# Expert results of a routed feed-forward layer: from one-hot scatter products and closing stores to accumulating indirect DMAs

## The reference, cut to what matters

```
def expert_choice_ffn(h, w_router, w_gate, w_up, w_down):
    ...
    aff = jax.nn.softmax((t @ w_router).astype(jnp.float32), axis=-1)
    gate, idx = lax.top_k(aff.T, cap)

    def expert(args):
        wg, wu, wd, ix, g = args
        xe = t[ix]
        he = jax.nn.silu(xe @ wg) * (xe @ wu)
        return (he @ wd) * g[:, None].astype(he.dtype)

    ye = lax.map(expert, (w_gate, w_up, w_down, idx, gate))
    y = jnp.zeros((n, D), h.dtype).at[idx.reshape(-1)].add(ye.reshape(-1, D))
...
x = x + expert_choice_ffn(rms_norm(x, norm2_g[l]), ...)
```

## Time and profile before

| | |
|---|---|
| median of 3 runs | 2422.82 us (2420.98 to 2423.57) |
| profiled execution, span | 2422.3 us |
| PE busy | 2308.2 us (95%) |
| PEld busy | 1983.5 us (82%) |
| DVE busy | 1764.9 us (73%) |
| ACT busy | 1390.5 us (57%) |
| POOL busy | 149.0 us (6%) |
| moved by DMA | 616.14 MB, 609.08 MB of it read from HBM |
| expert loop | from about 773 us to about 2404 us of the span |

### The profile page before, as it was taken

One profiled execution on the slowest core, in us unless ns is written; L12 is line 12 of the kernel. 1 busy time (PEld: TensorE's weight loads), 2 busy tenths in 40 slices (PEclk: granted clock), 3 DMA queues, 4 the chain that ended last, 5 costly groups with the idle time before them and its releaser, 6 DMA issues.

```text
span 2422.3 us, 32629 instructions
## 1 busy us (share of the span) xinstructions
PE 2308.2 (95%) x12576; PEld 1983.5 (82%) x12576; DVE 1764.9 (73%) x1571; ACT 1390.5 (57%) x1137; POOL 149.0 (6%) x119
## 2 busy tenths in 40 slices
PE   6899899999983999999999999999999999999998
PEld 4767778888773988888888888988889888898886
DVE  4456444223427988889888888888888888898886
ACT  3346346222222676766766677676676767767664
POOL 3301412000000000000000000000000000000000
PEclk9999999999985999999999999999999999999998
DMA  7120121112412999999999999999999999999995
GB/s 240 54 74 24 52 68 31 52 54 96 159 59 86 333 339 345 351 350 341 339 343 336 341 347 341 337 350 346 343 342 343 346 345 344 340 345 346 351 344 195
DMA packets 208240, 616.14 MB, mean 254 GB/s; under 512 B 10190, under 2 KB 10333, under 8 KB 208192
## 3 DMA queue, kind: packets, MB, share of 16 engines
q1 hardware_dynamic: 199648, 592.47, 68.3%
q0 software_dynamic: 8160, 22.19, 3.0%
q10 hardware_dynamic: 384, 0.82, 0.1%
HBM read 609.08 MB, written 12.40 MB: 257 GB/s over the span
## 4 chain that ended last, share of the span: by engine, by line
PE 81%; DVE 6%; ACT 5%; issue 4%; DMA 2%; POOL 1%; DVEq 0%; ACTq 0%; SPq 0%; POOLq 0%
PE PS L466 23%; PE PS L467 23%; PE PS L468 23%; ACT x_w_high L964 3%; PE PS L554 2%; DVE x_w_low L1039 2%; PE PS L717 2%; PE PS L566 2%; PE PS L718 2%; PE PS L769 1%; PE PS L578 1%; DMA small<-in_na_k_norm 1%; PE PS L486 1%; DVE hidden L1380 1%; PE PS L666 1%
## 5 line engine op out<-in xcount | busy, mean ns | idle before, releaser
L1039 DVE TENSOR_TENSOR x_w_low<-x_w_raw,x_w_high 128x2816 fp32r<-128x2816 f32 (+2 forms) x384 | 1185.9, 3088 | 195.9 <-ACT x_w_high L964 194.4
L964 ACT ACTIVATE x_w_high<-x_w_raw 128x2816 fp32r<-128x2816 f32 (+2 forms) x384 | 978.4, 2556 | 295.1 <-PE PS L468 292.4
L466 PE MATMUL PS<-x_w_high,xT_high 128*96 128x352 f32 x2048 | 669.1, 327 | 14.3 <-DVE x_w_low L1039 12.6
L468 PE MATMUL PS<-x_w_high,xT_low 128*96 128x352 f32 x2048 | 659.4, 322 | 0.0
L467 PE MATMUL PS<-x_w_low,xT_high 128*96 128x352 f32 x2048 | 659.2, 322 | 0.0
L466 PEld LDWEIGHTS PS<-x_w_high,xT_high 128*96 128x96 f32 x2048 | 330.6, 161 | 34.3 <-DVE x_w_low L1039 19.2
L467 PEld LDWEIGHTS PS<-x_w_low,xT_high 128*96 128x96 f32 x2048 | 332.9, 163 | 9.6
L468 PEld LDWEIGHTS PS<-x_w_high,xT_low 128*96 128x96 f32 x2048 | 332.0, 162 | 1.4
L466 PE MATMUL PS<-x_w_high,hidden_high 128*96 128x512 f32 x704 | 279.0, 396 | 0.0
L467 PE MATMUL PS<-x_w_low,hidden_high 128*96 128x512 f32 x704 | 278.4, 395 | 0.0
L468 PE MATMUL PS<-x_w_high,hidden_low 128*96 128x512 f32 x704 | 278.2, 395 | 0.0
(11 more groups left out here) (172 smaller groups left out, 2236.3 us busy)
## 6 DMA issues: line engine op xcount, KB each, us to landing
x_w_raw<-in_w_expert_gate SPq DMA_DIRECT2D x128, 1408.0 KB, 8.5
x_w_raw<-in_w_expert_up SPq DMA_DIRECT2D x128, 1408.0 KB, 8.6
x_w_raw<-in_w_expert_down SPq DMA_DIRECT2D x96, 1536.0 KB, 8.1
x_w_raw<-in_w_expert_down SPq DMA_DIRECT2D x32, 1024.0 KB, 7.2
w_raw<-in_w_in SPq DMA_DIRECT2D x20, 1024.0 KB, 5.1
x<-in_x_sample SPq DMA_DIRECT2D x8, 512.0 KB, 9.4
w_raw<-in_w_out SPq DMA_DIRECT2D x4, 1024.0 KB, 5.1
na_rep<-na_dram POOLq DMA_DIRECT2D x1, 3840.0 KB, 26.1
```

The lines of the kernel that those rows point to most:

```text
L466: mm(out, sh, mh, start=first, stop=False)
L468: return mm(out, sl, mh, start=False, stop=last)
L964: a_(xh[:, w % SPLITS, 0:n], xraw[:, w % RAWS, 0:n], ACT.Copy).then_inc(x_high, 1)
L1039: return v.tensor_tensor(out, src, high.bitcast(F32), ALU.subtract)
```

## The change

The scatter steps, the one-hot matrix, `y_low`, the adds into `x` and the closing stores go. Instead POOL stores each tile of `x` (the residual) to the outputs in HBM while the router's logits are made. ACT writes the gated result of an expert as one plain float32 tile `y_rows` (96 x 1024). POOL adds its rows to the outputs with two indirect DMAs whose operation is an addition: 64 rows into the sample output by the indices `idx_sample`, 32 rows into the prompt output by `idx_prompt`. It waits until both have landed before it lets go of `y_rows` (`ye_free`) and issues the next gather. ACT waits for `ye_free` before it writes; the count starts at 2, so that what it waits for is the scatter of two experts before.

```
-for _j, _w in enumerate([_w for _w in range(2, NXU) if _w not in MISC][:12]):
-    MISC[_w] = [("scatter", _j)]
...
-            for t in range(NT):
-                sp.wait_ge(S("x", "last_added"), 2 * t + 2)
-                sp.dma_start(xsrc(y_prompt, y_sample, t), xv[:, t, :]).then_inc(S("x", "stored"), 16)
-            sp.wait_ge(S("x", "stored"), 16 * NT)
...
+                pool.dma_start(xsrc(y_prompt, y_sample, t), xv[:, t, :]).then_inc(S("x", "residual_stored"), 16)
-            nc.gpsimd.iota(iota_tok, pattern=[[1, N]], base=0, channel_multiplier=0,
-                           allow_small_or_imprecise_dtypes=True).then_inc(S("x", "iota"), 1)
...
+            def scatter(e):
+
+                pool.wait_ge(S("x", "ye"), e + 2)
+                for y, rows, idx in ((y_sample, ye[0:CS, :], idxs), (y_prompt, ye[CS:CAP, :], idxp)):
+                    pool.indirect_dma_start(y, bass.IndirectOffsetOnAxis(ap=idx[:, e + 1:e + 2], axis=0), rows, None,
+                                            compute_op=ALU.add).then_inc(S("x", "scattered"), 16)
+                pool.wait_ge(S("x", "scattered"), 32 * (e + 1))
+                pool.sem_inc(S("x", "ye_free"), 1)
+
+            pool.sem_inc(S("x", "ye_free"), 2)
+            gather(0)
+            pool.dma_start(idxp, idxi[CS:CAP, :]).then_inc(S("x", "idxp"), 16)
+            pool.wait_ge(S("x", "misc"), PRE)
+            gather(1)
+            pool.wait_ge(S("x", "idxp"), 16)
+            pool.wait_ge(S("x", "residual_stored"), 16 * NT)
+            for b in range(E):
+                if b > 0:
+                    scatter(b - 1)
+                if b < E - 1:
+                    pool.wait_ge(S("x", "misc"), PRE + NU * b + use_no("tokens", 1) + 1)
+                    gather(b + 2)
+            scatter(E - 1)
...
-            def scatter(j, bank):
-                t, half = divmod(j, 2)
-                lhs = scat[:, t * P:(t + 1) * P]
-                cols = slice(half * 512, (half + 1) * 512)
-
-                mm(PS[:, bank, :], lhs, yeh[:, cols], start=True, stop=False)
-                mm(PS[:, bank, :], lhs, yel[:, cols], start=False, stop=True).then_inc(S("x", "misc"), 1)
...
-                        act.wait_ge(S("x", "cur"), e + 1)
-                        for half in range(2):
-                            i = a_(yeh[:, half * 512:(half + 1) * 512], PS[0:CAP, 4 + half, :], ACT.Copy,
-                                   scale=cur_g)
-                        i.then_inc(S("x", "ye_high"), 1)
+                        act.wait_ge(x_used, e * NXU + SPLITS)
+                        act.wait_ge(S("x", "ye_free"), e + 1)
+                        a_(ye.rearrange("p (h d) -> p h d", h=2), PS[0:CAP, 4:6, :], ACT.Copy,
+                           scale=gate_s[:, bass.ds(e, 1)]).then_inc(S("x", "ye"), 1)
...
+            v.tensor_scalar(idxs, idxf[0:CS, :], float(SP_), None, ALU.subtract)
+            v.tensor_copy(idxi, idxf).then_inc(S("rt", "tables"), 1)
...
-                slot_tables(e, e + 1)
...
-                        if what == "scatter":
-                            t, half = divmod(j, 2)
-                            dve.wait_ge(S("x", "misc"), e * NU + PRE + n + 1)
-                            xs = xv[:, t, half * 512:(half + 1) * 512]
-                            v.tensor_tensor(xs, xs, PS[:, 6 + n % 2, :], ALU.add).then_inc(S("x", "misc_read"), 1)
```

More of the change, by code:

```diff
@@ L104 @@
 PRE = 2
-NH_ = sum(m[0] != "scatter" for _, m in USES)
 def use_no(kind, i):
@@ L133, in encoder @@
         idxi = at("idxi", 904, E + 1, CAP, I32)
-        cur_f = at("cur_f", 928, 1, CAP)
-        cur_g = at("cur_g", 936, 1, CAP)
+        idxs = at("idx_sample", 928, E + 1, CS, I32)
+        idxp = at("idx_prompt", 43968, E + 1, CP, I32)
         xv = at("x", 960, NT * D).rearrange("p (t d) -> p t d", t=NT)
@@ L191, in encoder @@
         hidl = at("hidden_low", 28128, FT * CAP, dt=F32R)
-        yeh = at("y_high", 29184, D, CAP, dt=F32R)
-        yel = at("y_low", 30208, D, CAP, dt=F32R)
+        ye = at("y_rows", 30208, D, CAP)
         xraw = at("x_w_raw", 31680, RAWS * XUNIT).rearrange("p (b n) -> p b n", b=RAWS)
-        scat = at("scatter_onehot", 43968, N, CAP, dt=F32R)
         xe = at("gathered", 44736, D, CAP)
@@ L198, in encoder @@
         sg = at("silu", 47168, QF, CAP)
-        iota_tok = at("iota_tok", 47872, N, CAP)
         ident = cst[:, C_ID:C_ID + 128]
@@ L439, in _, with gather @@
             pool.wait_ge(S("rt", "tables"), 1)
[L442 to L446, removed]
+            def gather(e):
                 col = min(e, E - 1) + 1
@@ L762, in _ @@
                             transpose_tokens(j)
-                        elif what == "hidden":
+                        else:
                             h, r = divmod(j, 3)
@@ L771, in _ @@
                             i.then_inc(S("x", "misc"), 1)
[L772 to L783, removed]
         @block.scalar
@@ L1006, in expert_body @@
                     for what, j in MISC.get(u, []):
-                        if what != "scatter":
-                            n = use_no(what, j)
-                            misc_high(what, j, e * NU + PRE + n + 1, 6 + n % 2)
+                        n = use_no(what, j)
+                        misc_high(what, j, e * NU + PRE + n + 1, 6 + n % 2)
                     w = u + SPLITS
@@ L1018, in _ @@
             expert_body(E - 1, True)
-            act.wait_ge(S("x", "cur"), E + 1)
             act.wait_ge(x_used, NXU * E + SPLITS)
-            for half in range(2):
-                i = a_(yeh[:, half * 512:(half + 1) * 512], PS[0:CAP, 4 + half, :], ACT.Copy, scale=cur_g)
-            i.then_inc(S("x", "ye_high"), 1)
+            act.wait_ge(S("x", "ye_free"), E + 1)
+            a_(ye.rearrange("p (h d) -> p h d", h=2), PS[0:CAP, 4:6, :], ACT.Copy,
+               scale=gate_s[:, E:E + 1]).then_inc(S("x", "ye"), 1)
         @block.vector
@@ L1322, in _ @@
                                 ).then_inc(S("rt", "G"), 1)
-            v.memset(idxf[:, 0:1], -1.0)
+            v.memset(idxf[:, 0:1], 0.0)
             v.memset(gate_s[:, 0:1], 0.0)
-            v.memset(idxi[:, 0:1], 0)
             for half in range(2):
@@ L1335, in _ @@
             link(i)
-            v.tensor_copy(idxi[:, 1:E + 1], idxf[:, 1:E + 1]).then_inc(S("rt", "tables"), 1)
+            v.tensor_scalar(idxs, idxf[0:CS, :], float(SP_), None, ALU.subtract)
+            v.tensor_copy(idxi, idxf).then_inc(S("rt", "tables"), 1)
             dve.wait_ge(S("rt", "tables"), 1)
@@ L1347, in misc_low @@
                 low(dl[:, c0:c0 + w], PS[:, bank, 0:w], dh[:, c0:c0 + w]).then_inc(S("x", "misc_read"), 1)
[L1349 to L1364, removed]
             for q in range(PRE):
                 misc_low("tokens", q, q + 1, q + 1, 6 + q)
-            highs = [m for _, m in USES if m[0] != "scatter"]
             def expert_body(e, last):
-                slot_tables(e, e + 1)
                 for u in range(NXU):
-                    if u == 0:
-                        result_low(e + 1)
                     kind, q, c = XU[u]
@@ L1384, in expert_body @@
                         n = use_no(what, j)
-                        if what == "scatter":
-                            t, half = divmod(j, 2)
-                            dve.wait_ge(S("x", "misc"), e * NU + PRE + n + 1)
-                            xs = xv[:, t, half * 512:(half + 1) * 512]
-                            v.tensor_tensor(xs, xs, PS[:, 6 + n % 2, :], ALU.add).then_inc(S("x", "misc_read"), 1)
-                        else:
-                            misc_low(what, j, e * NU + PRE + n + 1, e * NH_ + PRE + highs.index((what, j)) + 1,
-                                     6 + n % 2)
+                        misc_low(what, j, n, e * NU + PRE + n + 1, 6 + n % 2)
                     w = u + SPLITS
@@ L1401, in _ @@
             expert_body(E - 1, True)
[L1402 to L1411, removed]
 _INS = ["x_prompt", "x_sample", "norm1_g", "w_in", "diff_q_norm", "diff_k_norm", "lambda_q1", "lambda_k1",
```

## The result

The changed kernel takes 2318.32 us (median of 4 runs, 2317.18 to 2319.50), the kernel before 2423.11 beside it: a ratio of 0.9567, 95% interval 0.9555 to 0.9579, 105 us or 4.3% faster. The forecast was 2330 with a range of 2301 to 2382.

A forecast was written before the change was run, and what follows sets the result against it. The prediction took PE's own work in the expert loop as the bound, DMA close behind. Span 2422.3 - 110 + 24 - 7 + 0.2 = 2329.5 us, with 0.5 to the median 2330; range for 8 in 10, 2301 to 2382.

The forecast's parts named there:

- The bound of the kernel before: In the expert loop, PE's own work binds the 101.7 us period; PE's waits are about 2.1 us, DMA close behind.
- A scatter step: Behind PE's units: 0.43 us after gate or up, 0.54 after down, 5.6 us for each expert, with nothing to hide it.
- The head of an expert: At each expert's start: PE's 1.6 us of waits fall to 0.25, as ACT writes `y_rows` right behind the table load.
- Sum on PE: Expert loop: 101.7 - 5.6 - 1.6 + 0.25 = 94.8 us for each expert, 6.9 less, 110 us in 16.
- What the loads give back: Weight loads in the loop: 0 to 3 us lost again per expert, middle 1.5 taken, 24 us in all; period 96.3.
- The signs to watch for: In the changed profile: ACT waiting for loads 10 to 30 us if the middle holds, over 50 if loads bind.
- The figure of the page: HBM to SBUF loads: at about 358 GB/s a core, period 100 us and loop gain 27; at 425, gain 110.
- The accumulates and the stores hide: On POOL's queue: accumulates of 10 or even 40 us hide in 99 us idle; residual stores beside the router cost nothing.
- The rival of a dear accumulate: DMA queues in the loop: at 2 us a row, six times the ordinary being 1.2, time 2494 us; chance 0.04.
- The rival of loads that bind already: Loop loads: extra bytes cost if the ceiling is under 352 GB/s; at 343, 2459 us; chance 0.05.
- The end: After the last product: 18.2 us of `y_low`, scatter steps, adds and stores become 11, saving 7 us (3 to 12).
- Span and median: Whole kernel: the median of the runs lies 0.5 us above the span, added to 2329.5 to give 2330 us.

The follow-up runs named there:

- the last run: Changed kernel with four buffers of split weights in place of three, and DVE making the splits of units 22 to 26 one unit later: 2304.73 us, ratio 0.9506.
- experiment one: Kernel before, with the loop's scatter steps left out on PE and DVE: 2354.31 us, ratio 0.9716.
- experiment two: Kernel before, with DVE's one-hot and copies of index and gate made three units earlier, nothing left out: 2402.66 us, ratio 0.9911.
- experiment five: Changed kernel, loading only half of each gate and up unit from the second expert on: 2315.68 us, ratio 0.9555.
- experiments four and seven: Changed kernel without the first 15 experts' accumulating DMAs: 2314.54 us; changed kernel with plain indirect writes in place of the additions: 2316.24 us.

## Why the prediction was right, point by point

- **The bound of the kernel before was PE's own work, with DMA close behind.** Right. The half loads show it for the changed kernel, the gain itself for the one before: PE's own work without any wait is 94.5 us (the last run), and with 5.6 of steps some 100.1 of the 101.7.
- **A scatter step costs PE 0.43 or 0.54 us, 5.6 for each expert, with nothing to hide it.** The price was right, the last clause not. Steps stood where PE would have waited for splits: some 0.7 us at the head and 0.8 in the middle of the expert. The steps alone bring 4.3 (experiment one). The sum named what covers an edit and did not ask what the removed work itself covered.
- **The head of an expert.** Right: 1.3 us as worked out (experiment two), `y_rows` directly behind the table load, unit 3 punctual, a wait of about 0.2 us at unit 4 where 0.25 was forecast. The activation of 1024 columns takes 1.11 us, 0.15 under the two of before.
- **Sum on PE, 94.8 us.** Measured 95.3. The missing part is the middle of the expert: the four down units there gave 1.5 us where 2.2 was priced. The shorter activation and small parts gave some of it back.
- **What the loads give back, 1.5 us for each expert.** This is the term that was mis-sized, 24 us in all: it measured 0 (experiment five). The ceiling taken from the best 30 us, 366 GB/s, was what PE asked for, not what the queues could give; they gave 371 over a whole period, and 377 when pressed. The working noted that no row told the two apart and took the middle. The landing times that it rested on did not grow: median 8.3 us at 342 GB/s, 8.4 at 371.
- **How near the forecast came.** It is 12 us too long, and that is less than its error of 24, by luck. The sum on PE promised 110 us and 102.0 came, the end promised 7 and 5.1 came: 10 us the other way. About 2.6 more lie between the profiled execution and the median.
- **The signs to watch for misled.** ACT waiting for loads in over 50 us was to mean that the loads bind, and waits turned from PE to the loads by more than 3 us an expert that the working was wrong. ACT waited 61.0 us, 3.8 an expert, and the loads did not bind: with these waits at 1.4 us the period is the same.
- **The figure of the page.** The Trainium skill's 358 GB/s for a core between HBM and SBUF ("DMA: Bandwidth & Descriptors", "Where 436 GB/s comes from") would have made the loads the bound at 100 us. The measured 377 over a period speaks against it as a limit of a core that runs alone; the same section's 425 was not reached either.
- **The accumulates and the stores hide.** Right (experiments four and seven). The rival of a dear accumulate fell: its bytes cost the queues about twice those of a load, where the rival needed six times. The working's count of them as two in 35.8 MB fits that, though the profile's 371 GB/s x 95.3 us = 35.4 MB has them once. The rival of loads that bind already fell with the half loads.
- **The end, 7 us less.** Measured 5.1, inside the 3 to 12 given, and for two reasons that cancel. The two DMAs land 4.7 and 4.1 us after their issues, sooner than most gathers did, so the last lands at 2309.3, 7.2 us behind the start of `y_rows`, where 11 was taken. The span ends 5.9 us later. The views list no instruction there, but the packed trace holds one of POOL's sequencer, a DRAIN from 2309.61 to 2314.98. It takes the same 5.37 us in every kernel that adds or writes one pair an expert, 2.92 without the loop's accumulates and 1.45 with four pairs; before, POOL's DRAIN (2.19 us) lay 116 us ahead of the end. What sets its length is open, and no term of the forecast had it.
- **Span and median.** The forecast added the 0.5 us between them before. In all runs with both on record the time of one execution is 1.7 to 2.1 us above its span; the 0.5 came of two different executions. The profiled execution of the changed kernel took 2317.18 us with a span of 2315.2.

## What to carry to other kernels

Before crediting removed work in full, look at what waited beside it: the part of it that stood inside another wait comes back, and the sum of two edits can be larger than their parts, as here 4.3 and 1.3 made 6.2. A rate read while another engine sets the pace is no ceiling; halving the bytes, which costs one run, tells whether transfers bind at all; neither a DMA share of 1.00 nor 61 us of waits for loads on ACT did. Nor is a wait in PEld's rows all gain when it goes: here 1.5 us of rows were 0.8 us of period. And where a small operation that others wait for stands behind long ones in an engine's order, move it: the same engine, the same work, and 21 us.

## What the runs showed of the hardware

The median time from issue to landing of the loads (1.0 to 1.5 MB each) was 8.3 us at 342 GB/s, 8.4 at 371 and 9.6 at 377 with four pairs; with the gate and up units halved it was 4.5 us. An accumulating indirect DMA of 96 rows of 4 KB, in two instructions, mostly keeps POOL 1.7 and 1.3 us. In the changed kernel its parts land 6.3 to 8.8 us after their issues in the midst of the loads, where a plain gather of as many rows takes 9.1 to 11.1, and 4.7 and 4.1 us behind the loads. Its bytes hold the DMA engines about twice as long as those of a load or of a plain write (84, 43 and 44 us for each MB). The gather's own time on POOL differed from kernel to kernel for the same instruction, 0.95 us in one and 2.95 in another of the three with four buffers; nothing waited for it, and its cause was not looked for.
